# First level of a block inverse as 64-row, 32-column products, and three groups of products in alternating head order

## The reference

```
def rwkv7_step(S, inp):
    r_t, dec_t, k_t, v_t, kk_t, a_t = inp
    sa = jnp.einsum('bhij,bhj->bhi', S, -kk_t)
    S = (S * dec_t[:, :, None, :]
         + sa[..., None] * (kk_t * a_t)[:, :, None, :]
         + v_t[..., None] * k_t[:, :, None, :])
    y = jnp.einsum('bhij,bhj->bhi', S, r_t)
    return S, y
...
    _, y = lax.scan(rwkv7_step, S0, seq)
```

## Time and profile before

| | |
|---|---|
| median of 3 runs | 2824.63 us (2813.09 to 2831.43) |
| the profiled execution | 2813.76 us, its span 2811.8 us |
| TensorE busy | 92% of the span |
| mean granted clock of TensorE | 0.946 |
| the recurrence's loop | about 1142 to 1380 us of the span |

### The profile page before, as it was taken

One profiled execution on the slowest core, in us unless ns is written; L12 is line 12 of the kernel. 1 busy time (PEld: TensorE's weight loads), 2 busy tenths in 40 slices (PEclk: granted clock), 3 DMA queues, 4 the chain that ended last, 5 costly groups with the idle time before them and its releaser, 6 DMA issues. The chain is left out here.

```text
span 2811.8 us, 32485 instructions
## 1 busy us (share of the span) xinstructions
PE 2599.0 (92%) x12202; PEld 2000.2 (71%) x12202; DVE 1166.3 (41%) x1995; ACT 947.6 (34%) x1616; POOL 1005.8 (36%) x606
## 2 busy tenths in 40 slices
PE   4997689999998989899799899999999898999997
PEld 3864447788883657778568678888866786888885
DVE  3002174411305475553262336426359733463362
ACT  3234464322326524222243332212323543322222
POOL 1430134544451222111046154434622461545344
PEclk9987779999999998888899999999999999999998
DMA  3220001233430110000133123323322331233231
GB/s 129 90 91 1 0 1 38 90 98 97 123 98 30 53 51 25 1 1 1 70 92 124 40 75 100 109 81 99 92 73 60 105 98 30 83 104 105 83 97 60
DMA packets 52108, 196.91 MB, mean 70 GB/s; under 512 B 6189, under 2 KB 6317, under 8 KB 51021
## 3 DMA queue, kind: packets, MB, share of 16 engines
q1 hardware_dynamic: 51008, 190.67, 21.7%
q10 hardware_dynamic: 974, 4.55, 0.5%
HBM read 193.10 MB, written 2.10 MB: 69 GB/s over the span
## 5 line engine op out<-in xcount | busy, mean ns | idle before, releaser
L486 POOL TENSOR_TENSOR w_lo<-raw,w_hi 128x1024 fp32r<-128x1024 f32 x342 | 818.9, 2404 | 1086.9 <-ACT w_hi L459 1086.7
L365 PE MATMUL ps<-ahead_hi,w_hi 128*128 128x512 f32 x1216 | 482.0, 396 | 1.1 <-DVE ahead_lo L588 1.1
L366 PE MATMUL ps<-ahead_lo,w_hi 128*128 128x512 f32 x1216 | 475.8, 391 | 0.0
L367 PE MATMUL ps<-ahead_hi,w_lo 128*128 128x512 f32 x1216 | 473.7, 390 | 0.0
L459 ACT ACTIVATE w_hi<-raw 128x1024 fp32r<-128x1024 f32 x342 | 353.1, 1049 | 217.3 <-PE ps L355 91.1
L365 PEld LDWEIGHTS ps<-ahead_hi,w_hi 128*128 128x128 f32 x1216 | 228.4, 188 | 54.5 <-issue 3.3
L367 PEld LDWEIGHTS ps<-ahead_hi,w_lo 128*128 128x128 f32 x1216 | 228.3, 188 | 50.9
L366 PEld LDWEIGHTS ps<-ahead_lo,w_hi 128*128 128x128 f32 x1216 | 228.5, 188 | 50.2 <-issue 3.1
L599 DVE TENSOR_TENSOR x_stream<-x_stream,ps 128x512 f32<-128x512 f32 x80 | 54.9, 687 | 466.6 <-PE ps L367 268.6
L353 PE MATMUL ps<-ffn_a_hi,w_hi 128*128 128x512 f32 x352 | 137.5, 390 | 2.9 <-DVE ffn_a_lo L2995 2.8
L354 PE MATMUL ps<-ffn_a_lo,w_hi 128*128 128x512 f32 x352 | 137.0, 389 | 0.0
(11 more groups left out here) (420 smaller groups left out, 4772.4 us busy)
## 6 DMA issues: line engine op xcount, KB each, us to landing
raw<-in_wall SPq DMA_DIRECT2D x346, 512.0 KB, 3.5
x_stream<-in_x SPq DMA_DIRECT2D x1, 2048.0 KB, 8.6
cw<-in_cmp_w SPq DMA_DIRECT2D x1, 2048.0 KB, 7.5
out_y<-x_stream SPq DMA_DIRECT2D x1, 2048.0 KB, 6.3
dist<-in_consts ACTq DMA_DIRECT2D x1, 1748.5 KB, 7.2
lora_a<-in_lora_a ACTq DMA_DIRECT2D x1, 1152.0 KB
mem<-in_mem SPq DMA_DIRECT2D x1, 1024.0 KB, 4.9
gwb<-in_lora_b SPq DMA_DIRECT2D x1, 1024.0 KB
```

The lines of the kernel that those rows point to most:

```text
L365: pe.matmul(out, hi, src.hi[:, t, 0:width], start=first, stop=False)
L366: pe.matmul(out, hi, src.lo[:, t, 0:width], start=False, stop=False)
L367: return pe.matmul(out, lo, src.hi[:, t, 0:width], start=False, stop=last)
L486: e.tensor_tensor(self.w.lo[:, s, :], self.raw[:, s, :], as_float(self.w.hi[:, s, :]), ALU.subtract).then_inc(lo_r.sem, 1)
```

## The change

Nothing outside five functions of the recurrence is touched, and no wait or semaphore. Which data flow where stays the same.

- `u32`: 8 matmuls with 128x128 weights and 64 columns streamed become 16 with 64x64 weights and 32 columns streamed, first on rows and columns 0 to 63, then on 64 to 127, in turn. Only blocks that are used later are computed.
- `t32`: 8 matmuls of 128x128 weights with 128 columns streamed become 16 of 64x64 weights with 32 columns streamed, in turn in the same way.
- `l32`: 32 columns streamed rather than 64; weights as before.
- `g_tensor` and `seed_y`: the same 8 matmuls each, in the order 0, 4, 1, 5, 2, 6, 3, 7 (`ORDER`) rather than 0 to 7. The output half of partitions, which is the column half of the array, so changes at every matmul rather than once.

```
@@ -2023,7 +2023,10 @@
         for q in range(8):
-            mm = pe.matmul(k.ps[:, 6, 64 * q:64 * q + 64], self.M[:, q, 0, :], self.Ta[:, q, :], start=True, stop=True)
+            for hh in range(2):
+                o, c = self.half(hh), 32 * hh
+                mm = pe.matmul(k.ps[o, 6, 64 * q + c:64 * q + c + 32], self.M[o, q, 0, o], self.Ta[o, q, c:c + 32],
+                               start=True, stop=True)
         done(mm, "u32")
@@ -2039,11 +2042,13 @@
         for q in range(8):
-            mm = pe.matmul(k.ps[:, 3 + q // 4, (q % 4) * P:(q % 4 + 1) * P], self.U[:, q, :], self.Tt[:, q, :],
-                           start=True, stop=True)
+            for hh in range(2):
+                o, c = self.half(hh), 64 * hh + 32
+                mm = pe.matmul(k.ps[o, 3 + q // 4, (q % 4) * P + c:(q % 4) * P + c + 32], self.U[o, q, o],
+                               self.Tt[o, q, c:c + 32], start=True, stop=True)
         done(mm, "t32")
         for q in range(8):
-            mm = pe.matmul(k.ps[0:64, 7, 64 * q:64 * q + 64], self.Tt[0:64, q, 0:64], self.U[0:64, q, 0:64], start=True,
+            mm = pe.matmul(k.ps[0:64, 7, 64 * q:64 * q + 32], self.Tt[0:64, q, 0:64], self.U[0:64, q, 0:32], start=True,
                            stop=True)
         done(mm, "l32")
@@ -2068,7 +2073,7 @@
     def g_tensor(self, pe, p):
-        for q in range(8):
+        for q in self.ORDER:
```

## The result

The changed kernel takes 2845.87 us (median of 8 runs, 2841.16 to 2849.31), the kernel before 2825.03 (8 runs). The ratio is 1.009, with a 95% interval from 1.0065 to 1.0114: slower by 0.9%. The profiled execution took 2841.32 us, 27.6 more than that of the kernel before.

The account below looks back on a forecast made before the run. TensorE bounds the kernel, through its work and its clock. Seven recurrence stretches at 25.0 us make 175 against 155.69; these 19 us more, put on the median, give 2844 us, range 2803 to 2866.

Parts of the forecast that it names:

- The groups: Changed matmul groups of the recurrence: at full clock `u32` 0.77 us, `t32` 0.81, `g_tensor` and `seed_y` together 1.08 less.
- The clock: Recurrence stretches: with `t32` small, nothing restores the clock before `g_tensor`, so 1.2 GHz until then; chance 0.62.
- The sum: Seven recurrence stretches, `u32` to `seed_y`: 25.0 us each, 175 together against 155.69, so 19 us more.
- the gain and the loss of the prologue: Prologue, mostly at 1.2 GHz already: shorter groups and lower clock were to be about even.
- Rival clock as before: Recurrence: only PE gaps lower the clock, any busy PE restores it; saves 21 us, 2803; chance 0.18.
- Rival no overlap of column halves: `g_tensor` and `seed_y` gain nothing from alternating column halves; 11 us above forecast, 2855; chance 0.12.
- Rival no overlap of quarters: `u32` and `t32`: 32 records run in a row, 3.8 us each at 1.2 GHz; 30 more, 2874; chance 0.08.
- the order's gain: `g_tensor` and `seed_y`: alternating column halves overlap, 0.54 us less each at full clock, from 1.51 to 0.97.
- use theory: Follow-up runs: the clock follows how much of the array's rows works; the change removes the only product restoring it.

Follow-up runs that it names:

- fill_after: Changed kernel plus two unread 128-row matmuls in TensorE's wait for DVE ahead of each `u32` but the first: 2789.07 us, 0.9892 of the kernel before.
- order: Kernel before with only the alternating order in `g_tensor` and `seed_y`: 2809.53 us, 0.9969 of the kernel before.
- t32_old: Changed kernel with the old `t32` back (8 products, 128x128 weights, 128 columns): 2826.58 us, 1.0035 of the kernel before.
- fill_before: Kernel before plus two unread 128-row matmuls in TensorE's wait for DVE ahead of each `u32` but the first: 2797.36 us, 0.9926 of the kernel before.
- fill_16rows: Kernel before plus two unread matmuls in the same wait ahead of `u32`, using only 16 rows: 2820.92 us, 1.0005 of the kernel before.
- products: Changed kernel without the alternating order, so only the small products of `u32`, `t32` and `l32`: 2839.63 us, 1.0081 of the kernel before.
- fill_order: Kernel before with the alternating order and two unread 128-row matmuls in the wait ahead of `u32`: 2800.37 us, 0.9928 of the kernel before.
- more: Changed kernel with two unread extra matmuls (identity weights, 512 columns) right behind `t32`: 2852.38 us, 1.0132 of the kernel before.
- fill_t32_old: Changed kernel with the old `t32` and two unread 128-row matmuls in the wait ahead of `u32`: 2799.2 us, 0.9927 of the kernel before.

## Why the prediction was right

The forecast was 2844 us, the measured median is 2845.87. Point by point:

- *The groups.* Forecast at full clock 1.07 for `u32` and 0.97 for `seed_y`, measured 1.06 and 1.03; at half clock 1.90 for `t32` and 1.9 for `g_tensor`, measured 1.73 and 1.91; `l32` 1.90 at half clock, measured 1.82. `l32` at full clock is 1.03 (1159.74 - 1158.71 in `fill_after`), 0.04 less than before: half the columns streamed gain nothing, as taken. The two quarters overlap in full (32 records in the time of 16), and `order` shows an overlap for column halves.
- *The clock.* It was forecast to stay at 1.2 GHz until `g_tensor`. From `ak_v` on at the latest it did in all seven stretches. Behind `g_tensor` it was to be back: it came back during `seed_sa` in four stretches, and in three it stayed low to the end. `t32_old` shows that in the loop the 128-row `t32` is what had brought it back (seven of seven with it, none of seven without), though it did not in the prologue, and `fill_before` against `fill_16rows` shows that rows count, not busy time alone. But the small `t32` is only one half of the loss. The forecast hung all of it on `t32` and took `u32` and `l32` to cost no clock; `t32_old` against `order` shows that those two together cost 17 us beside the old `t32`.
- *The sum.* A stretch was forecast at 25.0 us, its mean is 177.48 / 7 = 25.35. Errors partly cancel in it: `u32` was put at 1.90, at half clock, and ran at full clock in five stretches (mean 1.28, 4 us less over the seven), while `seed_sa` and `seed_y`, put at 1.93 and 0.97 at full clock, have means of 2.78 and 1.40 (9 us more). `t32` and `l32` took 1.73 and 1.82 rather than 1.90. The loop's loss between the stretches, 4.8 us, was not in the sum. That the median met the forecast to 2 us is partly luck: the profiled executions differ by 27.6 us, the medians by 20.8, and I had put 19. I had also put the gain and the loss of the prologue as about even, and they are: from its `u32` to the end of its `seed_y` 20.8 us against 21.3.
- *Rival clock as before*: false; its trigger point was the end of `t32`, and the clock was not back there. *Rival no overlap of column halves*: false by `order`. *Rival no overlap of quarters*: false, 32 records in 1.06 us at full clock.
- *What I had not seen*: that the order's gain exists only where it costs no clock. It is 7 to 9 us in `order`, and no gain is seen in the changed kernel or under the fill. The forecast counted it in the changed kernel too, at half clock: 0.9 us a stretch. The group is indeed that much shorter, and the time is given back by the later return of the clock. Four of my expectations by the use theory missed: `products` and `fill_order` on what the order is worth, `more` in its sign, `fill_t32_old` in its place. That less use of the array costs clock the runs show; how much of it, and where, the theory did not tell.

## What to carry to other kernels

Before a group of matmuls is made smaller, look at which clock the stretch runs and what came before each of its rises: the group may pay for the speed of all that follows. And try each part of such a change with the others in place and without them: the small `u32` loses beside the old `t32` (together with `l32`), and gains once the wait is filled. An unavoidable wait of TensorE was worth filling with useless matmuls that use all rows; the same time in 16-row matmuls did nothing. Here it was cheaper to keep the clock than to bring it back: the fill stands in a wait and costs next to nothing (the stretch at 1151 us starts 0.4 us later), while the extra work in `more` stands on the path and runs at half speed itself.

## What the runs showed of the hardware

- The granted clock depends on how much of the array is at work, not only on whether TensorE is busy: 1.98 us of 128-row matmuls in a wait changed the stretches from 155.69 to 138.34 us, 1.98 us of 16-row matmuls to 155.80. All rows are not enough either: 6.1 us of PE without a gap, in products of 128 rows with 64 columns streamed, were at half clock from end to end. Whether rows, cells or the data in them are what counts, these runs do not separate.
- Two 64x64 quarters on the diagonal run side by side even when each record streams only 32 columns: 32 records in 1.06 us at 2.4 GHz, 0.033 us each, half of the 0.06 that was the closest spacing in the trace of the kernel before.
- Streaming 32 rather than 64 columns through 64x64 weights saves next to nothing (1.03 against 1.07 us for 16 records).
- Two column halves in turn overlap though they share all rows: 16 records in 1.02 us against 1.51.
